# Second layer's feed-forward in folded form, weight sums on GpSimd

## The reference

```python
def _swiglu(h, w_in, w_out):
    a, b = jnp.split(h @ w_in, 2, axis=-1)
    return (jax.nn.silu(a) * b) @ w_out

xl = xl + ml[5] * _swiglu(_modulate(_rmsnorm(xl, norm_g[l, 1]), ml[3], ml[4]), w_ffn_in[l], w_ffn_out[l])
```

## Time and profile before

| | |
|---|---|
| median of 3 runs | 3082.83 us (3080.7 to 3086.12) |
| the profiled execution | 3084.4 us (its span from first to last instruction) |
| TensorE busy | 2925.2 us, 95% |
| VectorE busy | 1847.3 us, 60% |
| ScalarE busy | 821.4 us, 27% |
| GpSimd busy | 575.0 us, 19% |
| this feed-forward on TensorE | 2028.95 to 2262 us of the span |

### The profile page before, as it was taken

One profiled execution on the slowest core, in us unless ns is written; L12 is line 12 of the kernel. 1 busy time (PEld: TensorE's weight loads), 2 busy tenths in 40 slices (PEclk: granted clock), 3 DMA queues, 4 the chain that ended last, 5 costly groups with the idle time before them and its releaser, 6 DMA issues. The chain is left out here.

```text
span 3084.4 us, 37774 instructions
## 1 busy us (share of the span) xinstructions
PE 2925.2 (95%) x14236; PEld 2261.5 (73%) x14236; DVE 1847.3 (60%) x3960; ACT 821.4 (27%) x1905; POOL 575.0 (19%) x565
## 2 busy tenths in 40 slices
PE   7999999999999999999999999999999999888777
PEld 3888877758888888887998878888888744443222
DVE  3556675367775677644445557534236777777774
ACT  2132254311002100012123430010033454444443
POOL 2223321010000000103112100000000354344342
PEclk9999999999999999999999999999999999999999
DMA  6212211154432554544322234568534899999997
GB/s 244 93 63 69 69 42 61 50 170 125 135 123 76 157 153 134 167 137 124 110 83 83 69 107 153 173 240 318 196 120 138 310 420 420 420 421 420 421 416 323
DMA packets 278084, 582.23 MB, mean 189 GB/s; under 512 B 11720, under 2 KB 228936, under 8 KB 241552
## 3 DMA queue, kind: packets, MB, share of 16 engines
q0 software_dynamic: 51504, 338.98, 28.1%
q1 hardware_dynamic: 226400, 240.84, 24.1%
HBM read 578.70 MB, written 1.08 MB: 188 GB/s over the span
## 5 line engine op out<-in xcount | busy, mean ns | idle before, releaser
L4302 PE MATMUL banks<-weight_ring,work 128*128 128x512 f32 x512 | 249.3, 611 | 50.8 <-ACT work L4128 49.7
L4302 PE MATMUL banks<-work 128*128 128x512 f32 x512 | 250.7, 612 | 41.0 <-ACT work L4128 40.0
L436 DVE CUSTOM_DVE_ANT_0 work<-work 128x1024 f32<-128x1024 f32 x176 | 210.2, 1228 | 99.4 <-ACT branches L2830 46.9
L2608 PE MATMUL banks<-normed,weight_ring 128*128 128x256 f32 x1088 | 240.1, 384 | 6.7 <-ACT normed L2808 3.8
L2608 PEld LDWEIGHTS banks<-normed,weight_ring 128*128 128x128 f32 x1088 | 209.7, 193 | 36.5 <-ACT normed L2808 4.2
L3945 DVE CUSTOM_DVE_ANT_0 weight_ring<-weight_ring,branches 128x1024 f32<-128x1024 f32 x128 | 156.8, 1225 | 86.8 <-DMA weight_ring<-experts,branches 84.9
L4302 PEld LDWEIGHTS banks<-weight_ring,work 128*128 128x128 f32 x512 | 87.6, 189 | 161.2 <-ACT work L4128 98.2
L3945 DVE CUSTOM_DVE_ANT_0 work<-work,branches 128x1024 f32<-128x1024 f32 x128 | 156.8, 1226 | 77.4 <-DMA work<-experts,branches 72.0
L4302 PEld LDWEIGHTS banks<-work 128*128 128x128 f32 x512 | 87.6, 189 | 153.5 <-ACT work L4128 91.2
L406 POOL DMA_DIRECT2D work<-ada_turned x96 | 51.1, 533 | 772.3 <-DVEq L442 772.3
L3910 POOL DMA_INDIRECT weight_ring<-experts,branches x128 | 137.8, 1077 | 195.8 <-PE banks L4302 182.4
(11 more groups left out here) (653 smaller groups left out, 5595.4 us busy)
## 6 DMA issues: line engine op xcount, KB each, us to landing
weight_ring<-w_in SPq DMA_DIRECT2D x98, 1024.0 KB, 5.3
weight_ring<-w_ffn_in SPq DMA_DIRECT2D x44, 1024.0 KB, 5.2
work<-ada_turned POOLq DMA_DIRECT2D x80, 512.0 KB, 3.8
work<-ada_turned POOLq DMA_DIRECT2D x16, 1536.0 KB, 8.9
weight_ring<-w_ffn_out SPq DMA_DIRECT2D x18, 1024.0 KB, 5.4
weight_ring<-w_out SPq DMA_DIRECT2D x12, 1024.0 KB, 5.4
weight_ring<-w_br_ml SPq DMA_DIRECT2D x8, 1024.0 KB, 5.1
weight_ring<-w_br_da SPq DMA_DIRECT2D x8, 1024.0 KB, 5.2
```

What stands on the lines that cost most here:

```text
L436: last = dve.tensor_tensor_reduce(out=out, in0=slot[:, t, :], in1=self.rows[:, row, :], scale=1.0, scalar=0.0, op0=ALU.mult, op1=ALU.add, ...
L2608: ins = pe.matmul(bank(i)[:, 0:NLAT], w[:, k - at, half * P:(half + 1) * P], source[:, k, lat], start=k == 0, stop=k == total - 1)
L4302: last = pe.matmul(c.banks[2 * t + half][:], diag[:, r, :], vrows[r][:, half * 512:(half + 1) * 512], start=e == t * H * K, stop=e == (t + ...
```

## The change

`WAVE` stays. The other 20 chunks of `w_up` and three of the four chunks of `w_down` are multiplied in folded form, with halves of 128 tokens (`folded`). GpSimd makes the four weight sums of each (`mix_weights`, two buffers), VectorE the token sums (`mix_tokens`) and the unfolding (`unfold`), ScalarE copies the first product out of its bank (`copy_first`). The gate's and the value's chunk are now whole chunks of two tiles, so Silu and the product (`feed`) go by pairs. The conditioning tiles are loaded one by one by SyncE, between the weight chunks, and VectorE takes them in a fixed distribution: two beside each of nine chunks, one beside each of eleven, then 7, 7 and 5 ahead of the unfolding of the down chunks.

The core of the diff:

```diff
@@ Modulation.__init__ @@
+        if first is not None:
+            self.rows_loaded, self.rows_turn, self.loaded = c.rows_loaded_2, 1, c.ada_loaded_2
...
@@ latent_tail, sync @@
-            for chunk in range(2 * NF // 2):
+            for chunk in range(NF):
...
+                if chunk == SLOTS - 1:
+                    sp.wait_ge(c.merged, 2 * KT)
+                    condition(ADA_SLOTS)
+                elif chunk >= SLOTS + FIRST_UP:
+                    condition(BESIDE_UP_0 if chunk - SLOTS < UP_0 else BESIDE_UP_1)
...
+            beside = (1, 1, 1, 1, 2, 3, 2, 3, 2, 2, 2, 1)
...
                 load(chunk_of(w_down, 0, chunk, *cuts[cut]))
+                condition(beside[i])
...
@@ latent_tail, tensor @@
+            def folded(f, w, m, pairs, source, sums, wait_source, wait_sums, opens=True, closes=True, by_cut=False):
...
+                one(first, 0, part_of(w, 0, 0), tokens(0, 0), (True, False))
+                one(first, 1, part_of(w, 1, 0), tokens(1, 0), (False, False))
+                wait_sums()
+                pe.wait_ge(c.weights_mixed, 4 * m + 3)
+                last = one(first, 2, mixed[:, 1], token_mixture(1), (False, True))
...
+                one(second, 0, mixed[:, 0], token_mixture(0), (True, False))
+                one(second, 1, mixed[:, 2], token_mixture(2), (False, False))
+                pe.wait_ge(c.weights_mixed, 4 * m + 4)
+                one(second, 2, mixed[:, 3], tokens(1, 1), (False, False))
+                last = one(second, 3, part_of(w, 1, 1), token_mixture(3), (False, True))
...
-            for j in range(WAVE, 2 * NF):
...
-                product(B_UP + j, w, j % 2, c.h).then_inc(c.product, 1)
...
+            for f in range(N_UP):
+                folded(f, weights(), f, range(KT // 2), c.h, lambda i, pair: token_sums(i)[:, pair],
+                       lambda: None, lambda: pe.wait_ge(c.tokens_mixed, 1))
...
@@ latent_tail, vector @@
+            for f in range(N_UP):
...
+                unfold(f)
+                if f < UP_0 - FIRST_UP:
+                    condition(BESIDE_UP_0)
+                else:
+                    pair = f - (UP_0 - FIRST_UP)
+                    feed(f, pair)
+                    mix_tokens(lambda inputs, half: tokens_of(ffn, 2 * pair + inputs, half), lambda s: pair_sums(pair)[:, s])
+                    condition(BESIDE_UP_1)
+
+            for d in range(N_DOWN):
+                condition(BESIDE_DOWN[d])
...
+                unfold(f)
...
@@ latent_tail, gpsimd @@
+            def mix_weights(m):
...
+                pool.tensor_tensor(out[:, 0], part_of(w, 0, 1), part_of(w, 1, 1), ALU.add).then_inc(c.weights_mixed, 1)
+                pool.tensor_tensor(out[:, 2], part_of(w, 0, 0), part_of(w, 0, 1), ALU.subtract).then_inc(c.weights_mixed, 1)
+                pool.wait_ge(c.weights_mixed, 4 * m + 1)
+                pool.tensor_tensor(out[:, 1], out[:, 0], part_of(w, 0, 0), ALU.subtract).then_inc(c.weights_mixed, 1)
+                pool.wait_ge(c.weights_mixed, 4 * m + 3)
+                pool.tensor_tensor(out[:, 3], part_of(w, 1, 0), out[:, 1], ALU.subtract).then_inc(c.weights_mixed, 1)
...
-            for _ in loads:
-                pass
+            for m in range(N_UP + N_DOWN * len(cuts)):
+                mix_weights(m)
+                if m == N_UP + 2 * len(cuts) - 1:
+                    pool.wait_ge(c.squared, KT + 4)
+                    pairs(c.h, 0)
+                    pairs(c.mg, 0)
...
```

More of the change, by code:

```diff
@@ new lines, in _ @@
+            pe.wait_ge(c.folded_read, 4 * N_UP)
+            for cut, (k0, nk) in enumerate(cuts):
+                w = weights()
+                for half in range(2):
+                    last = product(B_LAST + 2 * N_DOWN + half, w, half, ffn, range(k0, k0 + nk), k0, NF)
+                    if cut == len(cuts) - 1:
+                        last.then_inc(c.product, 1)
+                if cut < len(cuts) - 1:
+                    last.then_inc(c.slot_used, 1)
+            sums_of_two(N_DOWN - 1)
@@ new lines, in feed @@
+            def feed(f, pair):
+                out = ffn[:, 2 * pair:2 * pair + 2, lat]
+                dve.wait_ge(c.folded_read, 4 * (f + 1))
+                dve.wait_ge(c.cleared, 3 * KT + 2 * (pair + 1) if pair < FIRST_UP else C_UP + pair - FIRST_UP + 1)
+                dve.tensor_tensor(out, out, spares[f % 2].rearrange("p (m t) -> p m t", t=NLAT), ALU.mult).then_inc(c.fed, 1)
+                dve.wait_ge(c.fed, pair + 1)
+            dve.wait_ge(c.moved, KT)
+            mix_tokens(lambda inputs, half: c.h[:, inputs:KT:2, NCTX + half * P:NCTX + (half + 1) * P], token_sums)
```

227 lines of the change are left out of this document (161 added, 66 removed).

## The result

The changed kernel takes 3101.05 us (median of 4 runs, 3094.62 to 3101.93), the kernel before 3084.47 beside it (4 runs, 3080.7 to 3087.2). The ratio is 1.005, with a 95% interval of 1.0034 to 1.0065: slower by 16.6 us where 10.1 were forecast. The profiled execution, 3094.62 us with a span of 3092.8, is the lowest of its four.

What follows compares the result with a forecast made beforehand. TensorE was taken to bound the second layer's feed-forward. Terms: -13.3 saved, +20.0 waiting for VectorE, +3.4 behind it, +10.1 in sum, so 3093 us by the median; own range 3088 to 3100, whole range 3070 to 3108.

Steps and rivals of the forecast that it cites:

- What bounds the kernel: Second layer's feed-forward, up and down products: TensorE busy without a gap, so a us saved there comes off the end.
- the chain that ended last: Second layer's feed-forward: cited as agreeing that TensorE bounds, since in this stretch it holds TensorE alone.
- TensorE's saving: Folded up tiles and three down chunks: 195.2 us of passes become 181.9 at 0.115 a pass, 13.3 us less.
- GpSimd's mix alone: Weight sums of each folded chunk: four additions last 5.1 us, hidden by TensorE's 6.44 if GpSimd is left alone.
- The port in turns: VectorE and GpSimd instructions with two SBUF inputs alternate: VectorE waits 3.0 us per chunk, 60 us over 20 chunks.
- The case of the earlier trace: A conditioning tile, 1.22 us alone, took 2.22 and let a second GpSimd addition pass.
- VectorE's account: First folded product to down chunk 0's residual: 3.2 start, 113.3 own work, 60 port, 5.3 loads, 181.8 us in all.
- TensorE's wait: Last up chunks, down chunk 0's last cut and its sums: 20.0 us, then 3.4 behind them.
- SyncE's queue: Last up chunks: it holds the next weights behind a conditioning load that waits for VectorE; part of the 20.0 us wait.
- GpSimd keeps the port for a whole mix: Rival: tiles let ready additions pass, 74 us of port waits instead of 60, 3107 us; chance 0.18 shared with unshortened passes.
- the passes don't shorten: Third rival: 128-column TensorE passes at 0.123 us, saving nil, 3104 us; chance 0.18 shared with GpSimd keeping the port.
- The saving: First rival: port waits 2.0 us or less per chunk, TensorE never waits, 3069.5 us; 2.5 about level; whole or mostly, 0.21.

Runs made afterwards that it cites:

- short_additions: Changed kernel with GpSimd's four additions per chunk cut to a quarter of the work, weight sums keeping old values: 3073.57 us, ratio 0.9970.
- sums_later: Changed kernel with all down chunks' sums of squares taken behind the last chunk's products, pair sums behind GpSimd's last mix: 3097.11 us, ratio 1.0044.
- By_cut_spread: Changed kernel with token sums in 12 additions instead of 44, residuals ahead of the conditioning tiles, and tiles spread anew with fewer late: 3087.30 us, ratio 1.0013.

## Why the prediction was right, step by step

- **The forecast as a whole: the sign and the mechanism right, the size in good part by luck.** The median, 3101.05, lies 1 us above the forecast's own range (3088 to 3100) and inside the whole one; the ratio on its base of 3082.83 gives 3098.2. How the terms came out is below.
- **What bounds the kernel: right, but the chain that ended last says nothing here.** Followed back, it ends at 2272.13, behind this stage, in the kernel before (and at 2276.50 in the changed one); that TensorE held the stage rests on the timeline without gaps alone.
- **TensorE's saving: right in kind, 13.3 was too small.** The earlier trace rows give 3.66 / 32 = 0.114 a pass, not 0.115, and with that 14.3. 20 folded up chunks take 125.06 us without gaps (short_additions), 6.25 each and 0.112 a pass; 138.2 became 125.1. The 462 passes of the three down chunks are 51.6 at that price, in place of 57.0. Together 18.5 us less.
- **GpSimd's mix alone, 5.1 us: right.** The first mix, with nothing of VectorE's beside it that has two SBUF inputs, went from 2013.45 to 2018.51.
- **The port in turns: right.** Of 48 tiles in the stage the longest took 2.35 us, 1.13 more than alone; none let two additions pass. That is what the Trainium skill has (SBUF — State Buffer, Who interferes with whom: the later one waits until the holder's instruction is through); the trace agrees in the order, the price is a little lower (a pair takes 1.68 us, not the 1.96 of both). The case of the earlier trace rows did not come back.
- **VectorE's account: its sum came out by luck, three terms did not.** Forecast 181.8 us from the first folded product to chunk 0's residual, measured 183.0 (2037.03 to 2220.0). The port cost about 45 in place of 60 (tiles 60.5 - 36 x 1.22 = 16.6, token sums 37.1 - 44 x 0.28 = 24.8, products of the halves 3.0, a bias addition 0.8); the loads 19.6 in place of 5.3 (10.4 at the seven tiles that were meant, 9.2 in up, where none was counted); the waits for TensorE at the start some 7 in place of 3.2. With 45 for the port and the rest as it stood, the prediction's own sum is -4.9, faster: 2.25 a chunk lies between its 2.0 for the whole saving and its 2.5 for level. The port's price a chunk is not a constant: it is what GpSimd leaves, 2.2 where it stood for weights (7.54 - 5.33) and 4.9 where it did not (10.28 - 5.33). Left out of what wants the port were the residuals of the folded chunks, which no longer read PSUM: the two of down chunk 1 took 1.59 us, those of chunk 0 0.88.
- **TensorE's wait: right in size, partly in place.** 20.0 up to chunk 0's sums and 3.4 behind them were forecast, 20.7 and 0.7 measured: 7.2 in up, 14.2 in the down part. Chunk 0's sums (7.8) and its last cut (0.7) are where they were named. That the gaps start in the sixth up chunk was not: I counted GpSimd's mix inside TensorE's chunk and charged the turns to VectorE alone. They stretch both sides, and at two tiles a chunk it is GpSimd that falls short, 7.0 against 6.25.
- **Put at nothing without a reason: the granted clock, and what a gap costs beside its idle time.** The folded up part is 9.5 us over its floor of 125.1; 7.2 are waits, and the other 2.3 come with its nine gaps, some 0.2 each beside the idle time (24 passes behind a gap take 2.92 us, 2.84 elsewhere). The three down chunks are 21.6 over 53.5, of which 14.2 are waits. Of the other 7.4 some 5.6 go with the clock (an estimate: TensorE was busy for 5.5 us from 2174.8 to 2181.6 and for 5.6 from 2223.8 to 2229.4, at a granted clock of 0.50 both times, and half of that is lost); 1.8 are left for the eight gaps. Behind the stage 4.1 us come with a clock of 0.94 in place of 1.00. That the change brings this one about is not shown: short_additions, with hardly a wait in the stage, has 0.94 and 817.0 us there, sums_later, with many, 1.00 and 813.7. These terms, and the larger saving the other way, are the difference between +10.1 and +16.6: -18.5, +9.5, +21.6, -1.4 (the four unfolded tiles, 15.3 us here and 154.9 - 138.2 = 16.7 before, at granted clocks of 0.91 and 0.83), +0.2 for the rest of the stage, +4.1 make +15.5.
- **SyncE's queue** was named as the place where lateness shows, and that is all it is: taken out of it, the loads cost time.
- **The rivals.** That GpSimd keeps the port for a whole mix is refuted by the tiles above, that the passes don't shorten by 0.112. The saving did not come through whole; what it is worth without the meetings short_additions shows: the stage 17.8 us shorter than before once GpSimd's instructions are short. The price of the third, 3104, does not follow from the prediction's own account: at 0.123 a pass TensorE reaches chunk 0's sums at 175.6 and waits 8.6, which makes some 3095.

What stays open: why no order with 29 whole mixes did better than level. By_cut_spread shows weights behind tiles and weight sums a little late; these were not taken apart further.

## What to carry to other kernels

Before GpSimd is given work beside VectorE, count the instructions with two SBUF inputs on both sides, not their lengths: each one that meets the other engine waits for most of one of the other's instructions, so many short ones cost most, and merging 44 into 12 with the same arithmetic was worth 11.6 us of the stage here, VectorE's own saving by it included. Both engines are stretched, so the slower of the two must still fit into TensorE's time per chunk. A late weight load can be the last link of a loop that starts at the engine that seems to be served: free the queue in an experiment before calling it the cause.

## What the runs showed that was not expected

- Where VectorE and GpSimd meet back to back, a turn costs a little less than both durations: a sum of 0.69 and an addition of 1.27 run at one pair per 1.68 us, not 1.96.
- Taking the loads out of SyncE's queue made the kernel slower: GpSimd without its pauses took 2.8 us more of VectorE's time per chunk (10.3 against 7.5), in two chunks more than before.
- The stage behind, which no kernel of this study changes, took 811 to 814 us where its first 60 us had a granted clock of 1.00 (five kernels with the one before), 815 to 816 at 0.97, 816 to 818 at 0.94 to 0.95 and 819 to 821 at 0.92. What sets that clock at its start was not found: the granted clock of the short stretch ahead of it was 0.84 both in the kernel before (then 1.00) and in the changed one (then 0.94).
